# Keeping four weight blocks on chip in place of four row buffers: a 12-place gather ring for a 16-place one

## The chip, the cores and the metric

One Trainium2 chip, of which the kernel uses one core. The core has a matmul engine (TensorE, PE in the profile), a vector engine (VectorE, DVE), a scalar engine (ScalarE, ACT), GpSimd (POOL) and SyncE (SP), and 16 DMA engines that move data between HBM and the on-chip memory. The metric is the device time in microseconds of one execution, lower is better. The time of a kernel is the median of its runs.

## The reference

512 tokens of width 1024 (and 16 meta tokens ahead of them) go through two blocks, all in float32:

```python
# first block
u = rmsnorm(h, ln_mix); z, xs, bs, cs, dt, sb, sc, sx, gates = split(u @ w_in)
y_ssd = ssd_branch(z, xs, bs, cs, dt, ...)          # chunked state-space scan, group norm, @ w_out
y_sc = (sb * causal_dwconv(sc * sx, conv_w)) @ w_out_sc
g = sigmoid(gates)
h = h + (g[..., :1024] * y_ssd + g[..., 1024:] * y_sc) @ w_o
# product-key experts: 8 heads x 16 of 16384 experts for every token
q = (xb @ w_q).reshape(T, 8, 2, 128); s = einsum('thjd,hjkd->thjk', q, sub_keys)
eidx, g = top 16 of the sums of the top 16 of either half, softmax
u = expert_u[eidx]; v = expert_v[eidx]              # (T, 8, 16, 1024) each
act = gelu(einsum('td,thkd->thk', xb, u)); h = h + einsum('thk,thkd->td', g * act, v)
# second block
q, k, v, f, u = split(rmsnorm(x) @ w_in_2)
attn = forgetting_attention(q, k, v, log_sigmoid(f)); pool = multiscale_pool(u)
x = x + concat(attn, pool) @ w_out_2
x = x + (silu(h2 @ w_gate_2) * (h2 @ w_up_2)) @ w_down_2; out = rmsnorm(x)
```

Each token needs its own 128 rows of `expert_u` and of `expert_v`, 4 KB a row. For a tile of 128 tokens these are 2 x 128 gathers of 128 rows (512 KB), so 1024 gathers for the four tiles.

## The kernel before

**Stages.** The tokens are four tiles of 128. The mixer (projections and scan) runs for tile 0 and then for tiles 1 to 3. The gated sum with `w_o` ("sum") and the query with the choice of experts ("choose") run for tile 0, for tile 1, and for tiles 2 and 3 together. The second block attends tiles 0 and 1, then 2, runs the feed-forward of tiles 0 to 2, and then attends and feeds tile 3.

**One list.** `make_plan` writes one list of units (`pl.units`) by costs and due times. Each engine's program walks this list in order and issues what is its own, so the order on each engine is fixed, and only semaphore waits move it in time.

**Weights.** `Plan.load` gives each weight load a slot: `ring` (four slots, `wr0` to `wr3`, taken in turn), `early` (three slots in the first part of the buffer `rows`, for the first query), and `last` (four slots in `rows`, free after the tile-3 gathers, for attending and feeding tile 3). SP issues the loads (L1144) strictly in list order; before each it waits until the slot's last user on PE is through (PE's product named `emptied` in the plan). So a load whose slot is still in use holds all loads behind it. The gate products of a sum ask for eight blocks `wgate` (1 MB each) in each of the three sums; those with index 0 and 1 are loaded three times. The attention's products ask for six blocks `wqku` (1 MB each), in each of the three attends.

**Rows.** The gathered rows land in `ring`, a view of places of 512 KB. POOL issues the 1024 gathers (L1172) in the order of their use: `dot` (VectorE multiplies a row of `expert_u` with the token and sums, L2745), `vrow` (VectorE adds a weighted row of `expert_v`, L2769; tiles 0 and 3), and `rows` (TensorE does the same for tiles 1 and 2 with 32-wide matmuls, L1200, one unit for four gathers). A gather waits until the earlier user of its place is done. The list `slots` sets which place comes next: at first 11 places in turn (7 to 10, 5, 6, 0 to 4), and from job `narrow` on, which is reached when the experts of tile 1 are chosen, all 16. A place therefore holds the data of a gather from its issue to its use, and POOL can be at most 11, later 16 gathers ahead of the engine that uses them.

In the profile L1172 is POOL's gather, L1144 SP's weight load, L1200 most matmuls, L2745 the dots and L2769 the weighted sums. `in_pu` and `in_pv` are the expert tables, `eidxT` marks the gathers for TensorE's sums, `in_wq` the query weights, `in_wso` the output weights of the two mixer branches.

Of the kernel before, what the change touches and what calls it, by code (L numbers as in the profile page):

```python
# [15 lines left out]
NT = 4  # L16
# [3 lines left out]
NEG = -3.0e38  # L20
NW = 4
NR = 16

VEC = {}
_o = 0
# [19 lines left out]
NR0 = 11  # L45
# [9 lines left out]
PIECES = (2, 4, 1)  # L55
# [57 lines left out]
class Plan:  # L113
# [2 lines left out]

    def __init__(self):
        self.units, self.bank, self.slot, self.loads = [], {}, {}, []
        self.held = {"ring": [], "early": [], "last": []}
        self.turns = ("ring",)  # L120
        self.rings = {"lo": (0, 1, 2, 3), "hi": (4, 5, 6, 7), "two": (2,), "five": (5,)}
        self.turn = {k: 0 for k in self.rings}
        self.use = [None] * 8
        self.p = self.v = 0.0
        self.stage = None
# [12 lines left out]
    def hold(self, key, i, emptied):  # L138
        self.bank[key] = (i, self.use[i])
        self.use[i] = emptied  # L140

    def load(self, key, src, n, emptied, place=None):

        if place is None:
            place = self.turns[len(self.loads) % len(self.turns)]
        held = self.held[place]
        k = len(held)
        first, n_ = {"ring": (0, NW), "early": (NW, 3), "last": (NW + 3, 4)}[place]
        old = held[k - n_] if k >= n_ else ("dve", "h2e", NT - 1) if place == "last" else None
        held.append(emptied)  # L150
        self.slot[key] = (first + k % n_, 16 * (k // n_ + 1))
        self.loads.append((key, src, n))
        self.add("load", len(self.loads) - 1, old)
# [200 lines left out]
def plan_sum(pl, A, q):  # L354
    nt, nr, off, first = columns_of(q)
# [2 lines left out]
        pl.add("ynorm", q, 1, v=nt * vc(256))  # L358

    def gate_products(j):  # L360
        pl.load(("wgate", q, j), A["wgate"][j], 2048, ("pe", "oprod", q, j, 1))
        pl.take(("oprod", q, j, 0), "hi", ("act", "gates", q, j))
        for k in range(2):
            pl.add("oprod", q, j, k, p=mmc(nr))
            if k == 0:
                yield True
        pl.add("gates", q, j)
        yield True
# [125 lines left out]
def plan_attend(pl, A, t0, t1):  # L494
# [12 lines left out]
        yield True  # L507

    def product(s3, s_):
        if s_ == 0:  # L510
            pl.load(("wqku", t0, s3), A["wqku"][s3], 2048, ("pe", "qku", t0, s3, 1))
        pl.take(("qku", t0, s3, s_), *(("lo", ("dve" if plain else "act", "qk", t0, s3, s_)) if s3 < 4 else
                                       ("hi", ("dve", "up", t0, 2 * (s3 % 2) + s_))))
        pl.add("qku", t0, s3, s_, p=mmc(nr))
        if s3 < 4 and not (plain and s3 == 0):
            pl.add("qk", t0, s3, s_)
# [50 lines left out]
    early = t1 == NT and nt == 1  # L567
# [277 lines left out]
def build(nc, A, out):  # L845
    with ExitStack() as ctx:
        sem = lambda n: ctx.enter_context(nc.semaphore(n))
# [1 line left out]
        sb = lambda n, s, d=F32: sbx(ctx, n, s, d)  # L849
        pe, act, dve = Count(sem("pe_done")), Count(sem("act_done")), Count(sem("dve_done"))  # L850
        counts = {"pe": pe, "act": act, "dve": dve}
        landed = [sem(f"weights_landed{i}") for i in range(NW + 7)]
        gathered = [sem(f"rows_landed{i}") for i in range(NR)]
        stored = [sem(f"stored{t}") for t in range(NT)]
        x_in = [sem(f"x_landed{t}") for t in range(NT)]
# [22 lines left out]
        rows = sb("rows", [128, NR * 1024])  # L878
# [116 lines left out]
            lay(m, arena, 0, first + small + rest + [("s_sb", [128, 16, 256]), ("oh", [128, 8, 256])])  # L995
        ob = ring[9:9 + NT]
        wr += [rows[:, WSLOT * i:WSLOT * i + WSLOT] for i in range(4)]
        with ExitStack() as pk:
            kT = st[:].rearrange("p a b -> p (a b)").rearrange("p (a b) -> p a b", a=4)
            vt = sbx(pk, "vt", [128, NT, 512])  # L1000
# [101 lines left out]
        for u in pl.units:  # L1102
            if u[0] in ("dot", "vrow"):
                jobs.append(u)
            elif u[0] == "rows":
                jobs += [("row", u[1], u[2], c) for c in range(4)]
        job_of = {u: i for i, u in enumerate(jobs)}
        consumers = ("dot", "vrow", "rows")
        narrow = NR0 + sum(4 if u[0] == "rows" else 1 for u in pl.units[:pl.units.index(("chosen", 1, 1, PIECES[1] - 1))]
                           if u[0] in consumers)  # L1110
        slots, user, slot_of, before_of, value_of = [7, 8, 9, 10, 5, 6, 0, 1, 2, 3, 4], {}, [], [], []
        for i in range(len(jobs)):
            if i == narrow:
                slots = list(range(NR0, NR)) + slots
# [1815 lines left out]
```

## Time and profile before

| quantity | value |
|---|---|
| time, median of 3 runs | 2383.35 us (2379.07 to 2385.44) |
| span of the profiled execution | 2541.9 us |
| TensorE busy | 2151.2 us, 85% of the span |
| VectorE busy | 1499.3 us, 59% |
| GpSimd busy | 1020.5 us, 40% |
| ScalarE busy | 653.7 us, 26% |
| bytes moved by DMA | 839.81 MB, mean 330 GB/s |
| of these weight loads on SP's queue | 290.72 MB |

The profiled execution is longer than the timed ones: its span of 2541.9 us stands against a median of 2383.35 us, a ratio of 0.938. Positions such as "at 1268 us" are on the clock of that profiled execution, from the start of its span. The stages lie on it roughly so: mixer of tile 0 to 420 us, mixer of tiles 1 to 3 to 835, sum and query of tile 1 to 1000, sum and query of tiles 2 and 3 to 1250 (with dots and sums of tile 1 beside them), the rest of tile 1's rows to 1417, the second block beside the dots and rows of tiles 2 and 3 to 2327, and the attention and feed-forward of tile 3 to the end.

### The profile page before, as it was taken

To read this page: it belongs to the slowest core of one execution; us is meant where nothing else is said; L and a number is where in the kernel's file an instruction comes from. 1 tells how busy PE (TensorE), PEld (TensorE's weight loads), DVE (VectorE), ACT (ScalarE), POOL (GpSimd) and SP (SyncE) were. 2 spreads that over 40 slices of the span, in tenths; PEclk is the share of its full clock that TensorE was granted. 3 is DMA by queue.
4 is the path that set the end of the run, shared out by engine and by line. 5 is a ranking of instruction groups with operands and counts; after the bars stand their busy time and mean duration, and the time that the engine had idled before them with its cause. 6 is when DMAs were issued, how large, how long until landed. Compare 5 with 4: busy or idle time off the path is not lost.

```text
span 2541.9 us, 29123 instructions
## 1 busy us (share of the span) xinstructions
PE 2151.2 (85%) x10694; PEld 1516.7 (60%) x10694; DVE 1499.3 (59%) x3505; ACT 653.7 (26%) x1838; POOL 1020.5 (40%) x1028
## 2 busy tenths in 40 slices
PE   8999998999999986996675366276879799999998
PEld 7999785666666975874431254221366555545695
DVE  3441179999999368647454677710067665886321
ACT  6772235566555121001010101110122000001220
POOL 0000014555665113435566554566544544772000
PEclk8999999999998997998886567578887899999999
DMA  6767568999999978999999888999978998998485
GB/s 237 245 231 240 215 254 298 404 397 393 390 377 337 378 274 320 398 356 380 363 394 361 308 335 320 366 343 364 409 307 323 411 348 313 412 412 355 157 316 173
DMA packets 196750, 839.81 MB, mean 330 GB/s; under 512 B 22000, under 2 KB 22384, under 8 KB 164864
## 3 DMA queue, kind: packets, MB, share of 16 engines
q0 software_dynamic: 147456, 536.94, 54.8%
q1 hardware_dynamic: 43808, 290.72, 30.6%
q10 hardware_dynamic: 5344, 10.29, 1.3%
q8 instruction: 85, 1.39, 0.2%
q14 instruction: 57, 0.47, 0.0%
HBM read 835.70 MB, written 2.16 MB: 330 GB/s over the span
## 4 chain that ended last, share of the span: by engine, by line
PE 60%; DVE 15%; issue 10%; ACT 6%; POOL 5%; another core or an unknown queue 3%; DMA 2%; ACTq 0%; DVEq 0%; SPq 0%
PE ps L1200 59%; DVE rows L2745 7%; POOL rows L1172 5%; DVE ps L2769 1%; DMA rows<-in_pv,eidxT 1%; DVE h L2769 1%; DVE arena L2297 1%; DMA wr<-in_wso 1%; ACT arena L1734 1%; ACT L1871 1%; ACT arena L1865 0%; DMA wr<-in_wgate 0%; ACT L1801 0%; DVE arena L2359 0%
## 5 line engine op out<-in xcount | busy, mean ns | idle before, releaser
L1172 POOL DMA_INDIRECT rows<-in_pu,eidx x512 | 485.3, 948 | 936.6 <-DVE dots L2745 368.7
L1200 PE MATMUL ps<-arena,wr 128*128 128x128 f32 (+4 forms) x3968 | 771.9, 354 | 26.0 <-DMA wr<-in_wso 9.2
L1200 PEld LDWEIGHTS ps<-arena,wr 128*128 128x128 f32 x3968 | 606.9, 195 | 168.6 <-issue 27.3
L2745 DVE CUSTOM_DVE_ANT_0 rows<-rows,ps 128x1024 f32<-128x1024 f32 x512 | 594.0, 1217 | 11.3 <-DMA rows<-in_pu,eidx 5.5
L1200 PE MATMUL ps<-hT,wr 128*128 128x128 f32 (+2 forms) x1600 | 369.7, 390 | 44.6 <-issue 41.3
L1172 POOL DMA_INDIRECT rows<-in_pv,eidx x256 | 289.2, 1130 | 207.0 <-DVE h L2769 101.4
L1200 PEld LDWEIGHTS ps<-hT,wr 128*128 128x128 f32 x1600 | 262.5, 199 | 148.7 <-issue 57.6
L1172 POOL DMA_INDIRECT rows<-in_pv,eidxT x256 | 245.7, 960 | 142.9 <-issue 68.6
L1200 PE MATMUL ps<-rows,wz 128*32 128x512 f32 x1024 | 180.7, 778 | 78.5 <-DMA rows<-in_pv,eidxT 57.1
L1200 PE MATMUL ps<-wr,arena 128*128 128x256 f32 (+2 forms) x704 | 180.7, 412 | 2.1 <-ACT arena L1943 2.1
L2769 DVE SCALAR_TENSOR_TENSOR h<-rows,wgt,h 128x1024 f32<-128x1024 f32 x132 | 169.0, 1280 | 5.7 <-DMA rows<-in_pv,eidx 4.8
L2769 DVE SCALAR_TENSOR_TENSOR ps<-rows,wgt,ps 128x1024 f32<-128x1024 f32 x122 | 156.6, 1284 | 8.1 <-DMA rows<-in_pv,eidx 8.1
L1200 PEld LDWEIGHTS ps<-wr,arena 128*128 128x128 f32 x704 | 129.5, 192 | 49.1 <-issue 33.7
L1200 PEld LDWEIGHTS ps<-rows,wz 128*32 128x32 f32 x1024 | 39.9, 129 | 198.1 <-issue 194.2
L1200 PE MATMUL ps<-wr,fT 128*128 128x512 f32 x304 | 135.2, 602 | 5.5 <-issue 5.5
L1200 PEld LDWEIGHTS ps<-wr,fT 128*128 128x128 f32 x304 | 58.5, 193 | 80.2 <-issue 80.2
L2297 DVE SCALAR_TENSOR_TENSOR arena<-arena,vec 128x144 f32<-128x144 f32 (+2 forms) x160 | 74.8, 468 | 51.9 <-ACT arena L1794 44.7
L2401 DVE TENSOR_TENSOR arena<-arena,ps 128x256 f32<-128x256 f32 (+1 forms) x24 | 12.3, 511 | 151.2 <-PE ps L1200 146.9
L2044 ACT ACTIVATE fT<-ps 128x384 f32<-128x384 f32 (+1 forms) x44 | 16.9, 385 | 276.9 <-PE ps L1200 145.5
L2681 DVE TENSOR_TENSOR fT<-fT,ps 128x384 f32<-128x384 f32 (+1 forms) x44 | 18.5, 421 | 112.7 <-PE ps L1200 86.3
L1200 PE MATMUL ps<-arena 128*128 128x64 f32 (+3 forms) x352 | 64.5, 314 | 11.8 <-DVE arena L2356 6.6
L2633 DVE CUSTOM_DVE_ANT_0 lg<-ps,cb 128x128 f32<-128x128 f32 (+3 forms) x32 | 15.7, 492 | 93.9 <-PE ps L1200 52.2
(403 smaller groups left out, 2258.3 us busy)
## 6 DMA issues: line engine op xcount, KB each, us to landing
wr<-in_wg SPq DMA_DIRECT2D x48, 1024.0 KB
wr<-in_wgu SPq DMA_DIRECT2D x33, 1024.0 KB
wr<-in_wgate SPq DMA_DIRECT2D x24, 1024.0 KB
wr<-in_wso SPq DMA_DIRECT2D x24, 1024.0 KB
wr<-in_wq SPq DMA_DIRECT2D x16, 1152.0 KB
wr<-in_wsc SPq DMA_DIRECT2D x16, 1024.0 KB
wr<-in_wqku SPq DMA_DIRECT2D x15, 1024.0 KB
wr<-in_wdn SPq DMA_DIRECT2D x14, 1024.0 KB
```

Source lines behind the costliest of these rows:

```text
L1172: e.indirect_dma_start(ring[slot_of[i]], None, A[table], bass.IndirectOffsetOnAxis(ap=index[:, t, k:k + 1], axis=0)).then_inc(gathered[slo ...
L1200: return e.matmul(o, l, r, start=start, stop=stop, skip_group_check=True)
L1734: e.activation(dst[:, kk, col:col + w_], b[:, 128 * k:128 * k + w_], ACT.Copy, scale=gv[:, kk:kk + 1]).then_inc(*act.up("turn", tag, s, half))
L1871: e.activation(m[f"mt{c % 2}"].rearrange("p a b -> p (a b)"), fall.rearrange("p a b -> p (a b)"), ACT.Exp, scale=-1.0).then_inc(*act.up("s ...
L2044: e.activation(FD[t0]["fT"][:, j, :], b[:, 0:nr], ACT.Silu).then_inc(*act.up("silu", t0, j))
L2297: e.scalar_tensor_tensor(out=tx[:, c1:n] if k < 3 else xg[:, s_, c1:n], in0=x[:, k + c1:k + n], scalar=W["convw"][:, q4 + k:q4 + k + 1], i ...
L2401: e.tensor_tensor(flat, flat, b[:, 0:2 * nr], MUL).then_inc(*dve.up("mg", q, j))
L2633: e.tensor_tensor_reduce(m[f"lg{p}"][:, 0:kn], b[:, 0:kn], cb[:, h, 0:kn], 1.0, NEG, ADD, ALU.max, mxx[:, p:p + 1]).then_inc(*dve.up("fron ...
L2681: e.tensor_tensor(fT[:, j, :], fT[:, j, :], b[:, 0:nr], MUL).then_inc(*dve.up("fT", t0, j))
L2745: e.tensor_tensor_reduce(row, row, wide[:], 1.0, 0.0, MUL, ADD, dots[:, k:k + 1]).then_inc(*dve.up(*u))
L2769: e.scalar_tensor_tensor(out=sum_, in0=row, scalar=wgt[:, k:k + 1], in1=sum_, op0=MUL, op1=ADD).then_inc(*dve.up(*u))
```

## The change

Two new slots (`kept`) are laid over places 7 to 10 of the row ring (`rows[:, 7168:11264]`). In them lie `wgate` 0 and 1, loaded once for all three sums, and, when the last sum has used them, `wqku` 0 and 1, loaded once for all three attends. The weight loads fall from 294 to 286; eight loads of 1024 KB are gone. For this the row ring gives up the four places: it runs over 7 places before `narrow` and over 12 after it. The index of the job `narrow` is 294 for 298. The fourth `last` slot lies over the first kept one, so its first load waits for the last product with `wqku` 0 and no longer for the norm ahead of tile 3.

```diff
+KEPT = 2
@@ class Plan
+    def keep(self, key, src, n, last):
+        first = (key[0], 0) + key[2:]
+        if first in self.slot:
+            self.slot[key] = self.slot[first]
+        else:
+            self.load(key, src, n, last, "kept")
@@ Plan.load
-        first, n_ = {"ring": (0, NW), "early": (NW, 3), "last": (NW + 3, 4)}[place]
-        old = held[k - n_] if k >= n_ else ("dve", "h2e", NT - 1) if place == "last" else None
+        first, n_ = {"ring": (0, NW), "early": (NW, 3), "last": (NW + 3, 4), "kept": (NW + 7, KEPT)}[place]
+        old = held[k - n_] if k >= n_ else None
+        if place == "last" and k < n_:
+            old = ("pe", "qku", NT - 1, 0, 1) if k == 3 else ("dve", "h2e", NT - 1)
@@ gate_products
-        pl.load(("wgate", q, j), A["wgate"][j], 2048, ("pe", "oprod", q, j, 1))
+        if j < KEPT:
+            pl.keep(("wgate", q, j), A["wgate"][j], 2048, ("pe", "oprod", 2, j, 1))
+        else:
+            pl.load(("wgate", q, j), A["wgate"][j], 2048, ("pe", "oprod", q, j, 1))
@@ product (attention)
-        if s_ == 0:
+        if s_ == 0 and s3 < KEPT:
+            pl.keep(("wqku", t0, s3), A["wqku"][s3], 2048, ("pe", "qku", NT - 1, s3, 1))
+        elif s_ == 0:
             pl.load(("wqku", t0, s3), A["wqku"][s3], 2048, ("pe", "qku", t0, s3, 1))
@@ the weight slots
         wr += [rows[:, WSLOT * i:WSLOT * i + WSLOT] for i in range(4)]
+        wr += [rows[:, 7168 + 2048 * i:7168 + 2048 * i + 2048] for i in range(KEPT)]
@@ the row ring
-        narrow = NR0 + sum(...)
+        narrow = NR0 - 2 * KEPT + sum(...)
-        slots, user, slot_of, before_of, value_of = [7, 8, 9, 10, 5, 6, 0, 1, 2, 3, 4], {}, [], [], []
+        slots, user, slot_of, before_of, value_of = [5, 6, 0, 1, 2, 3, 4], {}, [], [], []
```

The order of the computing instructions is the same on TensorE, VectorE and ScalarE, and so is the order of the 1024 gathers on POOL; the places of the gathers, and with them the waits, differ. What moves is SP's row of weight loads. On SP, in front of the query of tile 1 and the sum of tiles 2 and 3, before:

```order
L1144 DMA wr0<-in_wq 128x2304
L1144 DMA wr1<-in_wq 128x2304
L1144 DMA wr2<-in_wgate 128x2048
L1144 DMA wr3<-in_wq 128x2304
L1144 DMA wr0<-in_wq 128x2304
L1144 DMA wr1<-in_wq 128x2304
L1144 DMA wr2<-in_wq 128x2304
L1144 DMA wr3<-in_wgate 128x2048
L1144 DMA wr0<-in_wq 128x2304
L1144 DMA wr1<-in_wq 128x2304
L1144 DMA wr2<-in_wso 128x2048
L1144 DMA wr3<-in_wso 128x1024
```

and after:

```order
L1161 DMA wr0<-in_wq 128x2304
L1161 DMA wr1<-in_wq 128x2304
L1161 DMA wr2<-in_wq 128x2304
L1161 DMA wr3<-in_wq 128x2304
L1161 DMA wr0<-in_wq 128x2304
L1161 DMA wr1<-in_wq 128x2304
L1161 DMA wr2<-in_wq 128x2304
L1161 DMA wr3<-in_wq 128x2304
L1161 DMA wr0<-in_wso 128x2048
L1161 DMA wr1<-in_wso 128x1024
```

The two gate blocks of the coming sum no longer stand between the query's loads, and each query load takes a slot that comes free earlier. On SP, at the end of the query of tiles 2 and 3, before:

```order
L1144 DMA wr2<-in_wq 128x2304
L1144 DMA wr3<-in_wq 128x2304
L1144 DMA wr0<-in_wqku 128x2048
L1144 DMA wr1<-in_wqku 128x2048
L1144 DMA wr2<-in_wqku 128x2048
L1144 DMA wr3<-in_wqku 128x2048
L1144 DMA wr0<-in_wqku 128x2048
L1144 DMA wr1<-in_wqku 128x2048
```

and after:

```order
L1161 DMA wr0<-in_wq 128x2304
L1161 DMA wr1<-in_wq 128x2304
L1161 DMA rows<-in_wqku 128x2048 x2
L1161 DMA wr2<-in_wqku 128x2048
L1161 DMA wr3<-in_wqku 128x2048
L1161 DMA wr0<-in_wqku 128x2048
L1161 DMA wr1<-in_wqku 128x2048
```

The first two attention blocks go to the kept slots, which wait for nothing that is still to come, so six blocks are issued where four were before the ring was full.

## Rows read from the trace of the kernel before

**Rows 1.** Busy time by stretch: us, each engine (instructions), granted clock, DMA share, GB/s

```profile
420.00:840.00 420.00, 401.87 (x1685) 281.94 (x1683) 392.50 (x624) 240.85 (x694) 241.13 (x228) 0.97 0.99 384
938.00:1008.00 70.00, 40.68 (x244) 36.82 (x242) 57.59 (x210) 10.93 (x24) 32.36 (x34) 0.80 0.84 322
1310.00:1417.00 107.00, 61.92 (x312) 13.73 (x305) 61.06 (x293) 2.63 (x7) 74.97 (x75) 0.71 0.97 368
1640.00:1800.00 160.00, 107.31 (x531) 35.78 (x531) 22.79 (x67) 15.86 (x44) 102.03 (x109) 0.78 0.96 358
2160.00:2300.00 140.00, 139.24 (x377) 69.91 (x376) 120.25 (x104) 3.95 (x7) 104.14 (x91) 1.00 1.02 412
```

**Rows 2.** The page: the chain that ended last, shares of the span by engine

```profile
PE 60%; DVE 15%; issue 10%; ACT 6%; POOL 5%; another core or an unknown queue 3%; DMA 2%; ACTq 0%; DVEq 0%; SPq 0%
```

**Rows 3.** Gathers in 420 to 800 us: POOL's idle time before them, by releaser

```profile
  DVE dots L2745: 60.0, 54
  DVE h L2769: 45.9, 19
```

**Rows 4.** Order of time, VectorE, 424 to 440 us: start, duration, instruction

```profile
423.97 1.22 DVE L2745 CUSTOM_DVE_ANT_0 rows<-rows,ps 128x1024 f32<-128x1024 f32 x1
...
431.94 1.22 DVE L2745 CUSTOM_DVE_ANT_0 rows<-rows,ps 128x1024 f32<-128x1024 f32 x1
...
436.51 1.22 DVE L2745 CUSTOM_DVE_ANT_0 rows<-rows,ps 128x1024 f32<-128x1024 f32 x1
```

**Rows 5.** Order of time, POOL, from 1352.9 us: the last gather of a unit

```profile
1353.42 0.94 POOL L1172 DMA_INDIRECT rows<-in_pv,eidxT  x1 [0.30 <-issue]
```

**Rows 6.** Order of time, TensorE, from 1352.9 us: the unit that used it

```profile
1359.78 2.79 PE L1200 MATMUL ps<-rows,wz 128*32 128x512 f32 x12 [5.32 <-DMA rows<-in_pv,eidxT]
```

**Rows 7.** Order of time, TensorE, 938 to 1012 us, in tile 1's query

```profile
979.37 5.88 PE L1200 MATMUL ps<-rows,wr 128*128 128x128 f32 x32 [4.62 <-DMA wr<-in_wq]
...
996.69 3.72 PE L1200 MATMUL ps<-arena,wr 128*128 128x256 f32 x16 [1.07 <-DMA wr<-in_wso]
...
1008.00 4.32 PE L1200 MATMUL ps<-arena,wr 128*128 128x256 f32 x12 [6.70 <-DMA wr<-in_wso]
```

**Rows 8.** Order of time, TensorE, 834 to 850 us, at tile 1's sum

```profile
840.11 5.62 PE L1200 MATMUL ps<-arena,wr 128*128 128x128 f32 x48 [1.46 <-DMA wr<-in_wso]
846.43 3.84 PE L1200 MATMUL ps<-arena,wr 128*128 128x128 f32 x32 [0.69 <-DMA wr<-in_wgate]
```

**Rows 9.** Order of time, POOL, 1246 to 1275 us, gathers for TensorE's sums

```profile
1260.06 0.94 POOL L1172 DMA_INDIRECT rows<-in_pv,eidxT  x1 [0.53 <-remote]
...
1268.64 0.94 POOL L1172 DMA_INDIRECT rows<-in_pv,eidxT  x1 [3.90 <-PE ps L1200]
```

**Rows 10.** Order of time, TensorE, 1246 to 1275 us, tile 1's weighted sums (x16 is a unit)

```profile
1272.42 1.92 PE L1200 MATMUL ps<-rows,wz 128*32 128x512 f32 x16
```

**Rows 11.** Order of time, 1308 to 1322 us, both engines

```profile
1308.97 0.95 POOL L1172 DMA_INDIRECT rows<-in_pv,eidxT  x1 [7.40 <-PE ps L1200]
...
1314.56 3.48 PE L1200 MATMUL ps<-rows,wz 128*32 128x512 f32 x16 [2.47 <-issue]
```

**Rows 12.** Gathers in 1310 to 1410 us: who waited for them (us, times)

```profile
  PE ps L1200: 42.2, 15
```

**Rows 13.** SP's queue in order of time, 1236 to 1330 and 1500 to 1520 us

```profile
1238.79 12.23 SPq L1144 DMA_DIRECT2D wr<-in_wq  x2
...
1503.31 7.24 SPq L1144 DMA_DIRECT2D wr<-in_wqku  x2
```

**Rows 14.** Order of time, POOL, 1652 to 1680 us, tile 2's gathers

```profile
1664.65 0.94 POOL L1172 DMA_INDIRECT rows<-in_pv,eidxT  x1 [4.99 <-PE ps L1200]
...
1670.09 0.94 POOL L1172 DMA_INDIRECT rows<-in_pv,eidxT  x1 [0.77 <-PE ps L1200]
```

**Rows 15.** Order of time, TensorE, 1652 to 1680 us, tile 2's weighted sums

```profile
1675.52 1.92 PE L1200 MATMUL ps<-rows,wz 128*32 128x512 f32 x16
```

**Rows 16.** Weighted sums of tile 3, 2160 to 2330 us: VectorE's idle time before them

```profile
  DMA rows<-in_pv,eidx: 12.9, 11
```

More of the change, by code:

```diff
@@ L118, in __init__ @@
         self.units, self.bank, self.slot, self.loads = [], {}, {}, []
-        self.held = {"ring": [], "early": [], "last": []}
+        self.held = {"ring": [], "early": [], "last": [], "kept": []}
         self.turns = ("ring",)
@@ L851, in build @@
         counts = {"pe": pe, "act": act, "dve": dve}
-        landed = [sem(f"weights_landed{i}") for i in range(NW + 7)]
+        landed = [sem(f"weights_landed{i}") for i in range(NW + 7 + KEPT)]
         gathered = [sem(f"rows_landed{i}") for i in range(NR)]
@@ L1108, in build @@
         consumers = ("dot", "vrow", "rows")
-        narrow = NR0 + sum(4 if u[0] == "rows" else 1 for u in pl.units[:pl.units.index(("chosen", 1, 1, PIECES[1] - 1))]
+        narrow = NR0 - 2 * KEPT + sum(4 if u[0] == "rows" else 1 for u in pl.units[:pl.units.index(("chosen", 1, 1, PIECES[1] - 1))]
                            if u[0] in consumers)
-        slots, user, slot_of, before_of, value_of = [7, 8, 9, 10, 5, 6, 0, 1, 2, 3, 4], {}, [], [], []
+        slots, user, slot_of, before_of, value_of = [5, 6, 0, 1, 2, 3, 4], {}, [], [], []
         for i in range(len(jobs)):
```

## The prediction, made before the changed kernel was run

> **What bounds the kernel now.** I read the table of stretches first, to see which engine is full where. Between 420 and 840 us three things are full at once: TensorE 402 of 420 us, VectorE 393, and the DMA engines 99% busy at 384 GB/s. In tile 1's query (938 to 1008 us) TensorE is at 41 of 70 us. In the two stretches of weighted sums on TensorE (1310 to 1417, 1640 to 1800) it is at 58% and 67% while the DMA engines are at 0.97 and 0.96; from 2160 to 2300 us it is full again, 139 of 140, with VectorE at 120 [rows 1]. The chain that ended last agrees: PE has 60% of it, VectorE 15%, DMA as such only 2% [rows 2]. So the kernel is bound by TensorE where it is fed, and by the stream of gathered rows where TensorE sums them. Bytes count only where something waits for them, and so does the row ring's depth.
>
> Next come the waits at the ring. In 420 to 800 us POOL waited for a dot 54 times and for a weighted sum 19 times [rows 3]: the ring was full, and POOL as far ahead as it may be. That is what the change takes from.
>
> All terms below are in time of the profiled execution. Its span is 2541.9 us against a median of 2383.35, so a sum in the span is multiplied by 0.938.
>
> **How far ahead the ring must be.** A gather costs POOL 0.94 us and 0.30 us between two, 1.25 us in a row. The last of a unit's four was issued from 1353.42 to 1354.36 [rows 5], and the TensorE unit that waited for it started at 1359.78 [rows 6]: 5.4 us from the end of the issue to use. A place is thus out of use for at least 0.30 + 0.94 + 5.4 = 6.6 us. At the mean pace of the mixer stretch, 228 gathers in 420 us [rows 1] or 1.8 us a row, seven places are 12.5 us, and enough. In bursts they aren't quite.
>
> **The mixer, ring of 7 for 11.** The change takes four places for the kept gates from the start. At 424 us VectorE does eleven dots within 13.7 us: the first at 423.97, the seventh at 431.94, the last from 436.51 to 437.7 [rows 4]. With 11 places all eleven rows can lie ready. With 7, the eighth dot (433.1 us) needs the place of the first, free at 425.2: 425.2 + 6.6 = 431.8, which is in time by 1.3 us. The ninth to eleventh follow at POOL's 1.25 us, against 1.14 from dot to dot. The 5.4 us were measured in a stretch where few weights load. If landing takes 2 to 3 us more in the mixer, with DMA at 0.99, each burst stalls VectorE by 1 to 2 us, and VectorE idles only 27 of 420 us there [rows 1], so that a part of it reaches TensorE. The 228 rows of the stretch are some 20 such bursts; at a third of a us each that is 7 us. Low end 0 (all hidden), high end 20 (a full us each). I take +7, nearer to the low end, since the one burst that I can work out is covered.
>
> **The sum of tile 1: the kept gates.** TensorE waited 1.46 us for `wso` and 0.69 us for `wgate` there [rows 8]. With two of eight gate blocks already on chip SP's row is two loads shorter and both waits can go: −2 (−3 to 0).
>
> **The query of tile 1.** Two gate loads stand between the query loads, and four waits in turn hold them. TensorE waited 4.62 us for `wq`, 1.07 and 6.70 us for `wso` [rows 7]. Without the gates each query load takes a slot that is free one product earlier, so the first two waits should go. The last is a load that waits for a slot of a late query product, in the new order too; it stays. −5.7, and a little behind it: −6. High gain −12 (6.70 goes too), low 0 (a ScalarE result is what comes next).
>
> **Tile 1's weighted sums, ring of 12 for 16.** One unit uses four gathers, so POOL may be three units ahead for four. At 1260.06 POOL starts the four gathers of a unit, and at 1268.64, after a wait of 3.90 us for PE, those of the next [rows 9]. The wait at 1268.64 is for the fourth unit back. In the new ring the unit issued at 1260.06 waits for that same one, so it starts at 1268.64: its last gather is issued by 1268.64 + 3 x 1.25 + 0.94 = 1273.3 and is there at 1278.7. TensorE ran this unit at 1272.42 [rows 10]. +6.3. The same happens at 1308.97, where POOL had waited 7.40 us: the unit that TensorE starts at 1314.56 [rows 11] would be issued only from there, its last gather by 1313.7, there at 1319.1: +4.5. Behind it TensorE is already waiting for rows, 42.2 us in 15 waits [rows 12], and POOL issues without a pause; there the depth of the ring changes nothing more. A stream that goes from ahead to behind loses the four places once, 4 x 1.25 = 5.0 us, which is the size of both. Sum +10.8 (5 to 13).
>
> **Two more weight loads in the way.** The first two `wqku` blocks are issued right behind the query's last loads, which end at 1251.0 us; before, the last two of the six came at 1503 [rows 13], and now all six fall ahead of that. 2.1 MB at 368 GB/s [rows 1] are 5.7 us of the DMA engines just ahead of the stretch in which TensorE waits for rows. Taken at half, since gathers of POOL don't fill the engines by themselves: +3 (0 to 5.7).
>
> **Tile 2's dots and sums, and tile 3's.** Dots of tile 2: VectorE has slack; +2 (0 to 4). Sums of tile 2: at 1664.65 and 1670.09 POOL waits for PE [rows 14]. One unit's shift puts the unit used at 1675.52 [rows 15] behind the release at 1670.09: last issue by 1674.8, there at 1680.2, +4.7 (2 to 8). Tile 3's sums on VectorE already waited 12.9 us for rows in 11 waits [rows 16]; four places less cost it up to 5.0 us once, of which TensorE, 139 of 140 us busy [rows 1], sees what its next product that needs VectorE can't wait out: +4 (0 to 7).
>
> **The rest.** The four `wqku` blocks saved in the second and third attends were never waited for. The new wait of the fourth `last` slot holds only SP, with loads for tile 3's attention queued behind it, 10 us or more ahead of use: 0.
>
> Sum: 7 − 2 − 6 + 6.3 + 4.5 + 3 + 2 + 4.7 + 4 = **+23.5 us** of 2541.9, times 0.938 = +22.0: **2405 us**.
>
> **A page against a row.** The landing of 5.4 us decides five of the terms. The Trainium skill, "DMA: Bandwidth & Descriptors", section "Anatomy of one DMA — SWDGE (gpsimd) path", fits a transfer from GpSimd as 2.0 us plus bytes over 436,000 bytes per us; for 524,288 bytes that is an estimate of 3.2 us, and the rows show 5.4. By the page the ring of 7 would be ample. I stay with the row, which has this kernel's traffic in it. The rival "light rows" below is what a landing of about the page's size would do.
>
> **The rivals.**
> *Fewer bytes win (faster).* The DMA engines are at 0.96 to 1.02 in every stretch but the query [rows 1]; if transfers as such set the pace, 8 blocks of 1.05 MB, 8.4 MB at 384 GB/s, are 21.8 us less, half of it where rows are waited for. With the −8 of sum and query and no loss at the ring: −19, times 0.938: 2366 us. It decides if landing times shrink with the traffic so that 12 places carry what 16 did. Against it: four of the blocks go from stretches where no one waits for weights, the DMA engines moved 412 GB/s from 2160 to 2300 and 384 in the mixer, so that 384 is no ceiling, and the work at 1268.64 and 1308.97 waits by the order of units, not by traffic. Beside this, the same page, in "Where 436 GB/s comes from", puts the limit of HBM reads at about 358 GB/s a core; the 412 contradicts it as a ceiling here, and with it that every byte counts. Chance 0.10.
> *Even.* Landing is short in the mixer, VectorE's stalls stay on VectorE, and one of the two stalls in tile 1's sums is filled by other units: losses of 8 against gains of 8: 2383 us. Chance 0.15.
> *Light rows.* A row's landing is shorter where the stream isn't behind: midway between the 1.3 us that 0.52 MB take at 412 GB/s and 5.4, so 3.3 us. Then tile 1's stalls are 4.2 and 2.4, tile 2's 2.6, tile 3's 2, the mixer's and the dots' 0, the early blocks 3: −8 + 14.2 = +6.2, times 0.938: 2389 us. Only the one row of 5.4 speaks against it. Chance 0.07.
> *The mixer stalls in earnest.* Landing there takes 8 us or more; the pace of seven places is then (8 + 1.2 + 1.2) / 7 = 1.5 us a row, each burst loses over 1 us, and TensorE follows: +20 for +7, the other terms at their upper ends (13, 5.7, 4, 8, 7) less 8: +50, 2430 us. Chance 0.16.
> *The forecast*, 2393 to 2420 us: chance 0.52.
>
> **How the numbers follow.** About 0.3% is what a measurement of this kernel can tell from no change: 2376 to 2390. Faster by more is the first rival, with the lower edge of the even case: 0.11. Within it: the even case, light rows and no more, less that edge: 0.20. Slower: forecast and stalling mixer, 0.69. For 8 in 10 the range runs from 2379, just under the even case, to 2432, just over the stalling mixer; what is left out is the fast rival below and the worst tenth above.
>
> **What would show it.** In the new profile: POOL's waits for PE around 1250 to 1310 grow from four short ones to one a unit, and TensorE waits for `rows<-in_pv,eidxT` there two times, some 5 us each (right), or its busy share in the stretch stays (wrong). VectorE gets waits for `rows<-in_pu` in 420 to 840, about 10 us in all; none at all means the mixer term is 0. The waits of 4.62 and 1.07 us for weights in tile 1's query vanish and that of 6.70 stays. The prediction is wrong in sign if the stretches of weighted sums take no longer while the query loses its waits, and wrong in size mainly through the landing time in the mixer.

## The result

The changed kernel takes 2435.72 us (median of 4 runs, 2426.5 to 2439.56) against 2383.76 us before: a ratio of 1.021, 95% interval 1.0184 to 1.0237, so 52 us slower. The forecast was 2405 us with a range up to 2432. The sign was right; the size was less than half of what was measured, and the time lies outside the range. One of the four runs of the kernel with only the early ring cut, told of below, took 2827.79 us at a granted clock of 0.726 and is left out of every number here.

### A second profile of before

The execution profiled for [rows 1] to [rows 16] was 158 us longer than its timed runs. A second profile of the same program has a span of 2378.2 us, and its timed runs agree (2383.64 us, ratio 1.0013, 0.9992 to 1.0034). It is the one to lay beside the changed kernel. The page of the second profile of before: the span, the busy time by engine, and the chain that ended last.

```profile
span 2378.2 us, 29123 instructions
...
PE 2077.9 (87%) x10694; PEld 1480.3 (62%) x10694; DVE 1501.1 (63%) x3505; ACT 652.3 (27%) x1838; POOL 1016.5 (43%) x1028
...
PE 54%; DVE 20%; DMA 9%; issue 6%; POOL 6%; ACT 6%; ACTq 0%; DVEq 0%
```

The page of the changed kernel, the same lines:

```profile
span 2437.7 us, 29111 instructions
...
PE 2101.6 (86%) x10694; PEld 1491.3 (61%) x10694; DVE 1507.9 (62%) x3505; ACT 651.4 (27%) x1838; POOL 1013.1 (42%) x1028
...
PE 46%; DVE 23%; DMA 14%; POOL 6%; ACT 6%; issue 5%; ACTq 0%; DVEq 0%
```

Busy time hardly moved; waiting did. The chain has 14% of its length in DMA for 9%, and 23% in VectorE for 20%. The first profile showed only 2% for DMA [rows 2]. Two things differ there. TensorE was slower (busy 2151 us for 2078), and its idle time before the units that sum rows was shorter. And that trace holds no landing time for any of the 1024 gathers, so a part of the waits for rows stands under other names: its chain has 10% "issue" and 3% "another core or an unknown queue", where the second profile has 6% and none. The groups of these units in the first and in the second profile (busy, mean ns | idle before):

```profile
L1200 PE MATMUL ps<-rows,wz 128*32 128x512 f32 x1024 | 180.7, 778 | 78.5 <-DMA rows<-in_pv,eidxT 57.1
L1200 PE MATMUL ps<-rows,wz 128*32 128x512 f32 x1024 | 157.7, 745 | 98.5 <-DMA rows<-in_pv,eidxT 97.3
```

The idle time itself is 78.5 us for 98.5; only 57.1 of the 78.5 was put down to rows. The waits of the second profile of before, over the whole span (engine, what it waited for: us, times, longest):

```profile
PE ps L1200 <- DMA rows<-in_pv,eidxT: 97.3, 43, 8.1
POOL rows L1172 <- PE ps L1200: 44.2, 23, 6.1
DVE rows L2745 <- DMA rows<-in_pu,eidx: 35.5, 29, 3.4
```

and of the changed kernel:

```profile
PE ps L1217 <- DMA rows<-in_pv,eidxT: 105.8, 44, 8.1
POOL rows L1189 <- PE ps L1217: 64.8, 31, 6.2
DVE rows L2762 <- DMA rows<-in_pu,eidx: 49.2, 38, 3.4
```

So VectorE and TensorE waited for rows before the change too, in more places than the first profile let see, and a shorter ring makes POOL wait more (44.2 to 64.8 us behind TensorE) and the users of the rows too.

### Where the time went

VectorE has the same 3505 instructions in the same order in all kernels here, so the start of one and the same instruction can be compared between traces. The growth of each stretch over the second profile of before, in us (the third column is the ring of the changed kernel with the loads of before, the next two cut one ring only; they are told of below):

| stretch (us in the second profile of before) | changed | ring 7, 12 | early 7 | late 12 | forecast |
|---|---|---|---|---|---|
| mixer, tiles 1 to 3 (414 to 807) | +17.0 | +15.9 | +16.9 | 0.0 | +7 |
| sum and query of tile 1 (807 to 1017) | −2.4 | −1.3 | −1.7 | −3.8 | −8 |
| tile 1's dots beside the next sum (1017 to 1144) | +8.1 | +10.5 | +9.6 | +3.4 | none |
| tile 1's sums on TensorE (1144 to 1376) | +10.4 | +5.1 | −3.5 | +3.6 | +10.8, +3 |
| tile 2's dots (1376 to 1563) | −1.2 | +8.1 | +0.2 | +8.5 | +2 |
| tile 2's sums (1563 to 1774) | +6.5 | +6.5 | +0.2 | +6.4 | +4.7 |
| 1774 to 1998 | +16.1 | +7.0 | +9.3 | +14.3 | none |
| tile 3's sums on VectorE (1998 to 2192) | +7.4 | +9.3 | +0.4 | +8.4 | +4 |

The rest lies within 2.4 us at the start and 0.0 at the end. In the mixer these profiles agree well: all kernels with 7 places and full loads have +15.9 to +17.1, all with 11 have 0.3 us or less. The stretch from 1774 us on needs a word: +16.0 of its +16.1 come between 1799 and 1851 us, where TensorE's granted clock dips. The kernel with only the early ring cut has a like dip and +9.3 us there, though its ring is the full one by then, so 9.3 of the 16.1 are taken to be the clock. Its trace by tens of us (each engine's busy time, granted clock, DMA share, GB/s), in that place:

```profile
1822.00:1832.00 10.00, 10.00 (x31) 6.71 (x30) 5.26 (x15) 3.25 (x9) 2.67 (x4) 0.50 0.99 394
1832.00:1842.00 10.00, 9.13 (x41) 8.54 (x41) 6.58 (x15) 2.18 (x6) 3.13 (x4) 0.50 0.64 199
```

and the second profile of before:

```profile
1810.00:1820.00 10.00, 9.12 (x28) 4.47 (x28) 9.74 (x20) 2.08 (x3) 6.73 (x8) 1.00 1.02 406
1820.00:1830.00 10.00, 10.00 (x35) 6.37 (x34) 8.60 (x16) 1.15 (x2) 6.57 (x7) 1.00 1.02 417
```

The granted clock is 0.50 there, the lower level of 1.2 GHz, for 24 us, against 1.00. Beside the first profile there are thirteen: nine have the dip for 24 to 27 us, two for 7 us (one of them is the kernel of the third column), two not at all. The first profile of before has it for 27 us and the second, of the same program, has none, so it is not fixed by the program; what sets it off is open. The timed runs of the kernel before scatter by 20 us with a granted clock from 0.924 to 0.938. Less 9.3 us the changed kernel's profile is 50 us longer, near the 52 of the timed runs.

### The profile page after: what moved, and what is told of

The parts are those of the page before. It is cut to its first block, busy times and chain, and to the rows that moved or that the text cites. A ratio compares the mean times of both kernels' runs of the same rounds, so it can differ in the third digit from the quotient of the medians.

```text
span 2437.7 us, 29111 instructions
## 1 busy us (share of the span) xinstructions
PE 2101.6 (86%) x10694; PEld 1491.3 (61%) x10694; DVE 1507.9 (62%) x3505; ACT 651.4 (27%) x1838; POOL 1013.1 (42%) x1028
## 4 chain that ended last, share of the span: by engine, by line
PE 46%; DVE 23%; DMA 14%; POOL 6%; ACT 6%; issue 5%; ACTq 0%; DVEq 0%
PE ps L1217 45%; DVE rows L2762 12%; POOL rows L1189 6%; DMA rows<-in_pu,eidx 5%; DMA rows<-in_pv,eidxT 4%; DMA rows<-in_pv,eidx 4%; DVE h L2786 1%; DVE arena L2314 1%; DVE ps L2786 1%; DMA wr<-in_wgate 1%; ACT arena L1751 1%; DVE rows L2226 1%; ACT L1888 0%; ACT arena L1882 0%; DVE rows L2224 0%
## 5 line engine op out<-in xcount | busy, mean ns | idle before, releaser
L1217 PE MATMUL ps<-arena,wr 128*128 128x128 f32 (+4 forms) x3776 | 740.5, 356 | 17.5 <-DMA wr<-in_wso 10.1
L1217 PEld LDWEIGHTS ps<-arena,wr 128*128 128x128 f32 x3776 | 577.3, 194 | 158.6 <-issue 17.9
L2762 DVE CUSTOM_DVE_ANT_0 rows<-rows,ps 128x1024 f32<-128x1024 f32 x512 | 601.8, 1217 | 53.2 <-DMA rows<-in_pu,eidx 49.2
L1217 PE MATMUL ps<-hT,wr 128*128 128x384 f32 (+2 forms) x1440 | 323.1, 385 | 5.7 <-DVE fT L2698 4.2
L1217 PEld LDWEIGHTS ps<-hT,wr 128*128 128x128 f32 x1440 | 228.2, 192 | 97.4 <-DVE fT L2698 4.8
L1217 PE MATMUL ps<-rows,wz 128*32 128x512 f32 x1024 | 163.9, 770 | 107.1 <-DMA rows<-in_pv,eidxT 105.8
L2786 DVE SCALAR_TENSOR_TENSOR ps<-rows,wgt,ps 128x1024 f32<-128x1024 f32 x122 | 156.7, 1284 | 13.7 <-DMA rows<-in_pv,eidx 13.6
L1217 PE MATMUL ps<-hT,rows 128*128 128x128 f32 (+1 forms) x608 | 84.8, 301 | 21.1 <-DVE xx L2612 20.4
L1217 PEld LDWEIGHTS ps<-hT,rows 128*128 128x128 f32 x608 | 79.8, 203 | 24.5 <-issue 18.6
L2061 ACT ACTIVATE fT<-ps 128x384 f32<-128x384 f32 (+1 forms) x44 | 16.9, 384 | 261.9 <-PE ps L1217 201.2
```

Source lines behind the costliest of these rows:

```text
L1217: return e.matmul(o, l, r, start=start, stop=stop, skip_group_check=True)
L2061: e.activation(FD[t0]["fT"][:, j, :], b[:, 0:nr], ACT.Silu).then_inc(*act.up("silu", t0, j))
L2762: e.tensor_tensor_reduce(row, row, wide[:], 1.0, 0.0, MUL, ADD, dots[:, k:k + 1]).then_inc(*dve.up(*u))
L2786: e.scalar_tensor_tensor(out=sum_, in0=row, scalar=wgt[:, k:k + 1], in1=sum_, op0=MUL, op1=ADD).then_inc(*dve.up(*u))
```

## The experiments

### Which ring, and what the kept blocks give

The ring of the changed kernel, with the old loads, leaves places 7 to 10 unused:

```diff
-        narrow = NR0 + sum(...)
-        slots, ... = [7, 8, 9, 10, 5, 6, 0, 1, 2, 3, 4], ...
+        narrow = NR0 - 4 + sum(...)
+        slots, ... = [5, 6, 0, 1, 2, 3, 4], ...
```

> The row ring of the changed kernel (7 places, then 12) with the weight loads of the kernel before; the four places lie unused. Theory A (the lost places cost more than I had them, the kept blocks give back about 8 us): slower than the changed kernel, 2440 to 2450 us, +57 to +65 over before. Theory B (the ring costs the 22 to 30 us that I had, and the loss beyond it comes from the kept blocks: early attention blocks in the way of the rows, or the order of the loads): 2405 to 2415 us, well under the changed kernel's 2436.

Measured: 2447.11 us, ratio 1.0281 (1.0258 to 1.0305), +64. Theory A, near its upper end.

Cutting the early ring alone adds places 7 to 10 back at `narrow` (`slots = list(range(NR0 - 4, NR)) + slots`):

> Only the early ring is cut, 7 places for 11; the late one has all 16, the loads are those of before. By my sum the mixer's term alone: +7 us of span, 2390 us. Theory A with the mixer mis-sized: +15 to +20 us, 2400 us. If the early ring is long enough (its places wait less than the dots need): 2384 us.

Measured: 2409.5 us (three runs), ratio 1.0112 (1.0081 to 1.0144), +26. More than either number that I had.

Cutting the late ring alone takes them out there (`+ [s for s in slots if s not in (7, 8, 9, 10)]`):

> Only the late ring is cut, 12 places for 16; the early one has its 11, the loads are those of before. By my sum 6.3 + 4.5 + 2 + 4.7 + 4 = 21.5 us of span, about 2404 us. Theory A with the late terms mis-sized: +35 to +45 us, 2420 to 2430 us. If only one of the two cuts matters, this and the run with the early ring cut tell which; if their losses add up to that of both cuts, the stages don't share it.

Measured: 2421.22 us, ratio 1.0171 (1.0148 to 1.0195), +38. The losses add up: 26 + 38 = 64 for 64. The kept blocks give back 2447.1 − 2435.7 = 11 us beside the short rings. The second profile of before, for the record of the expectation:

> The kernel before once more, for a second profile of it. The first profiled execution was 158 us longer than its timed ones; this one should show where. Every theory expects a ratio of 1.000 within 0.2%. If the profiled span is near 2382 us, it is the one to lay beside the changed kernel's 2437.7.

It came out at 2378.2 us of span, as told above.

### What the kept blocks give by themselves

The kernel before with its full rings, and no transfer for the eight repeated loads; their products read a constant tile instead, so its output is of other numbers:

```diff
+        if j < 2 and q > 0:
+            pl.slot["wgate", q, j] = (NW + 7, 0)
+        else:
             pl.load(("wgate", q, j), A["wgate"][j], 2048, ("pe", "oprod", q, j, 1))
...
+        if s_ == 0 and s3 < 2 and t0 > 0:
+            pl.slot["wqku", t0, s3] = (NW + 7, 0)
+        elif s_ == 0:
             pl.load(("wqku", t0, s3), ...)
...
+        wr.append(Same(con))
```

> The gain side by itself. The kernel before with its full rings (11, then 16 places), in which the eight repeated loads are simply left out: the products of gate blocks 0 and 1 in the second and third sums, and of attention blocks 0 and 1 in the second and third attends, take their weights from a constant tile instead (so those products are of other numbers; nothing else differs). Theory A (a saved transfer is worth only what someone waited for): the query's waits of 4.4 and 1.2 us and part of the sum's 3.3, 2378 to 2381 us, -4 to -7. Theory B (bytes count, since the DMA engines are full): 8.4 MB at 400 GB/s are 21 us, half or more of which shows, 2363 to 2373 us. If the waits only move to the next load: 2384 us.

Measured: 2379.35 us, ratio 0.9986 (0.9968 to 1.0005): −3 us, no change that can be told. Theory A fits, and so does "the waits only move"; the interval, +1 to −8 us, leaves both. Theory B (−11 us or more), and with it my rival "fewer bytes win", falls. So on the full rings, with memory that costs nothing, the kept blocks could bring 8 us at the very most. The waits of TensorE for weights in tile 1's query say why. In the second profile of before:

```profile
959.15 5.46 PE L1200 MATMUL ps<-rows,wr 128*128 128x128 f32 x32 [4.38 <-DMA wr<-in_wq]
...
976.22 3.72 PE L1200 MATMUL ps<-arena,wr 128*128 128x256 f32 x16 [1.24 <-DMA wr<-in_wso]
...
988.45 23.82 PE L1200 MATMUL ps<-arena,wr 128*128 128x256 f32 x97 [7.62 <-DMA wr<-in_wso]
```

and in the changed kernel:

```profile
994.62 5.70 PE L1217 MATMUL ps<-arena,wr 128*128 128x256 f32 x17 [8.97 <-DMA wr<-in_wso]
```

The first two waits are gone, as forecast from [rows 7], and the third stayed and took up 1.3 us more. 13.2 us of waiting became 9.0. At tile 1's sum nothing was won: three waits of 3.3 us together in the second profile of before, three of 2.5 in the changed kernel and of 2.4 with the same ring and the old loads.

Keeping the gates only, and giving their places back to the ring once the last sum has used them (7, then 11, then 16 places):

```diff
+        mid = NR0 - 2 * KEPT + sum(... units before ("oprod", 2, 1, 1) ...)
...
+            if i == mid:
+                slots = [7, 8, 9, 10] + slots
```

> Half of the change: the two gate blocks are kept, the attention blocks are loaded as before, and the four places go back to the row ring as soon as the last sum has used the gates (7 places, then 11, then 16). By the parts so far: +27 of the early ring less what the kept gates give, which the profiles put at 3 to 4 us in tile 1's query (waits of 4.4, 1.2 and 7.6 us for weights become one of 9.0): 2405 to 2409 us. If the gates' 4 MB less traffic counts by itself in the mixer and the sums, 2395 us or less. If returning the places earlier than the choice of tile 1's experts matters, 2400.

Measured: 2403.31 us, ratio 1.008 (1.0054 to 1.0106). That is 6 us better than the early ring cut alone, though the intervals overlap, so the stretches must tell; its mixer is +17.1 like the others', and the dots from 1017 to 1144 us are at −0.1 where all the others with 7 places have +6.5 to +10.5. So that second loss, which my sum did not have, is the short ring too. It is an after-effect. The wider ring begins with the job `narrow`, whose gather is issued at 1022.9 us in the second profile of before and within 2 us of that point of VectorE's work in the others, while the loss comes from 1037 to 1090 us. But the early ring sets how far ahead POOL is when the long run of gathers begins. Job 288 is issued at 999.0 us with 11 places, at 1009.3 on the same clock with 7, and at 999.7 with the places handed back. Behind `narrow` POOL issues a gather every 1.25 us almost without a pause, and until it is ahead again VectorE waits. Its idle time before these dots (us, times), in the second profile of before, with 7 early places, and with the places handed back:

```profile
  DMA rows<-in_pu,eidx: 5.4, 5
  DMA rows<-in_pu,eidx: 13.0, 9
  DMA rows<-in_pu,eidx: 1.9, 2
```

### Why seven places are too few

Two places more:

> An early ring of 9 places (between the 7 that cost 27 us and the 11 of before), 16 later, loads as before. If the loss is proportional to the places: half, 2397 us. If 11 is well over what is needed and 7 just under it (bursts of dots longer than the ring), most is won back by two places: 2385 to 2390 us. If the ring is still too short at 11, the loss is nearly linear or more, 2395 to 2400.

Measured: 2392.39 us, ratio 1.0032 (1.0008 to 1.0056), +8 of the 26. By this interval (+2 to +13 us) alone half the loss could not be told from a quarter. The stretches can tell: in the mixer it is +1.3 us for +16.9, and from 1017 to 1144 us +1.2 for +9.6. In these two stretches the loss is not proportional to the places; there is a knee between 7 and 9. The chain of the changed kernel, followed back through its mixer, starts with these pieces (start, us, what):

```profile
413.10 9.72 DMA rows<-in_pu,eidx
422.85 1.22 DVE rows L2762
424.35 9.87 DMA rows<-in_pu,eidx
434.25 1.22 DVE rows L2762
```

A row takes 9.7 and 9.9 us there from the start of its gather; from the end of the gather, as I had measured 5.4 [rows 5, 6], that is 8.8 and 8.9. Nine places' worth of dots at 1.14 us are 10.3 us, about what such a row needs; seven, 8.0 us, are not. To see whether the weights' traffic makes the rows late, the mixer's weight loads for tiles 1 to 3 were halved, in the kernel before and in the one with 7 early places (the other half of each block is left out, so the products read there what the slot held before):

```diff
+                    if key[0] in ("wg", "wsc") and key[1] == 1:
+                        n //= 2
+                        src = src[:, 0:n]
                     e.dma_start(wr[slot][:, 0:n], src).then_inc(landed[slot], 16)
```

> The pair for the next run: the kernel before, but the mixer's weight loads for tiles 1 to 3 bring only the first half of their columns (the products read what was there before in the other half, so the numbers differ; instructions and waits are the same). Stage from the first dots in the mixer to its end (393.0 us in the second profile of before): all theories expect 390 to 393 us, since nothing waited for these loads.

> The kernel with an early ring of 7 places, with the same halved weight loads. The stage was 17 us longer than before with full loads. Theory L (7 places are too few because a row lands late, behind the weights' traffic; a place's round is landing plus 2.4 us, and 7 rounds of 10 to 12 us are at or over the 1.8 us a row that the stage takes): with half the weights the rows land earlier and the growth over the pair falls to 0 to 6 us. Theory P (POOL's pace of one gather in 1.25 us after each burst limits, whatever the landing): the growth stays at 13 to 17 us.

Measured, one execution of each, in the stretch from the mixer's first dots to its end: 392.8 us with 11 places and 398.8 with 7, a growth of 6.0 us where full loads gave 16.9. Two thirds of the loss went with half of the weights: theory L, at the top of its bounds. Whether the 6 us left are the other half of the weights or something else is not shown. The gathers of the dots in the first 190 us of that stretch (count, median us from the start of the gather to landing; the traces hold the landing of about half of them or more) say the same. Before, second profile:

```profile
rows<-in_pu,eidx POOLq DMA_INDIRECT x106, 10.2
```

seven early places with full loads, and then with half loads:

```profile
rows<-in_pu,eidx POOLq DMA_INDIRECT x110, 9.0
```

```profile
rows<-in_pu,eidx POOLq DMA_INDIRECT x108, 6.7
```

VectorE's idle time before the dots there (us, times), with full loads and with half:

```profile
  DMA rows<-in_pu,eidx: 8.0, 10
```

```profile
  DMA rows<-in_pu,eidx: 0.5, 1
```

With 11 places a landing of 10.2 us is longer than with 7, and does no harm: VectorE has no wait for rows there. With 7 places it falls to 9.0, and still VectorE waits. Over the whole mixer the changed kernel's VectorE waits 8.7 us for rows before dots and 3.9 before weighted sums, both from nothing.

### The late ring, and the two loads ahead of tile 1's rows

> A late ring of 14 places between the 12 that cost 38 us and the 16 of before. Proportional: 2402 us. The sums on TensorE use four places a unit, so 14 places let POOL be three units ahead and half of a fourth. If whole units decide, 14 is little better than 12 for tiles 1 and 2: 2410 us; if rows decide, 2395 to 2402.

Measured: 2394.17 us, ratio 1.0036 (1.0018 to 1.0055), +9 of the 38. Half the places cost a quarter of the loss (the interval is +4 to +13 us); it bends as well, less sharply. That is the reading "rows decide", just under its 2395; whole units do not.

In the changed kernel TensorE waits for the first rows of this stretch right behind the new `wqku` loads (order of time, TensorE's sums in the changed kernel):

```profile
1253.06 3.64 PE L1217 MATMUL ps<-rows,wz 128*32 128x512 f32 x16 [4.93 <-DMA rows<-in_pv,eidxT]
1258.18 3.32 PE L1217 MATMUL ps<-rows,wz 128*32 128x512 f32 x16 [1.48 <-DMA rows<-in_pv,eidxT]
1263.30 1.92 PE L1217 MATMUL ps<-rows,wz 128*32 128x512 f32 x16 [1.80 <-DMA rows<-in_pv,eidxT]
1268.42 1.92 PE L1217 MATMUL ps<-rows,wz 128*32 128x512 f32 x16 [2.11 <-DMA rows<-in_pv,eidxT]
```

With only the late ring cut, and the old loads, the same units:

```profile
1229.64 3.08 PE L1200 MATMUL ps<-rows,wz 128*32 128x512 f32 x16 [3.20 <-DMA rows<-in_pv,eidxT]
1234.76 3.64 PE L1200 MATMUL ps<-rows,wz 128*32 128x512 f32 x16 [2.04 <-DMA rows<-in_pv,eidxT]
```

10.3 us of waits for 5.2. To test it, the kept blocks became the last two of the six, loaded when tile 1's sums are over:

```diff
-        if s_ == 0 and s3 < KEPT:
-            pl.keep(("wqku", t0, s3), A["wqku"][s3], 2048, ("pe", "qku", NT - 1, s3, 1))
+        if s_ == 0 and s3 >= 4:
+            pl.keep(("wqku", t0, s3), A["wqku"][s3], 2048, ("pe", "qku", NT - 1, s3, 1), ("pe", "rows", 1, 31))
```

> The changed kernel, but the two attention blocks that are kept are the last of the six (4 and 5) instead of the first, and they are loaded only when TensorE has done tile 1's last sum, not right behind the query's loads. If the two extra megabytes in front of tile 1's row stream cost what the profiles say (8.0 us of growth from 1220 to 1266 us against 3.2 with the old loads), this is 4 to 5 us faster than the changed kernel: 2430 to 2432 us. If the growth there has another cause: 2436 us. If the later load is missed at the start of the attention, slower.

Measured: 2444.21 us, ratio 1.0264 (1.0237 to 1.0292): 8 us slower than the changed kernel by the medians, with intervals that just touch, and in no case faster. The local part held: from 1144 to 1376 us the growth is 4.5 us for the changed kernel's 10.4, near the 5.1 of the short rings with the old loads. But tile 2's dots, which cost the changed kernel nothing, now cost 7.9 us, as in the two kernels with a short late ring and the old loads (8.1 and 8.5). What was won in one place was given back in the next. In the kernel with only the late ring cut VectorE waits for the dots' rows there, and SP brings four blocks within some 40 us (SP's queue, order of time; the second `wqku` at 1442.57, the second `wv` at 1456.4):

```profile
1415.49 27.41 SPq L1144 DMA_DIRECT2D wr<-in_wqku  x2
1449.48 7.23 SPq L1144 DMA_DIRECT2D wr<-in_wv  x2
```

and the idle time before the dots from 1440 to 1473 us:

```profile
  DMA rows<-in_pu,eidx: 5.9, 4
```

The changed kernel has its six attention blocks by then, and only the two `wv` loads fall there:

```profile
1478.04 7.24 SPq L1161 DMA_DIRECT2D wr<-in_wv  x2
```

The kernel just told of has four blocks again. Its attention blocks come early, but the rest of SP's queue moves up behind them: one `wv` at 1438.92 us, then, within 14 us, the other (1463.0) and two `wout`:

```profile
1438.92 24.43 SPq L1163 DMA_DIRECT2D wr<-in_wv  x2
1469.92 7.24 SPq L1163 DMA_DIRECT2D wr<-in_wout  x2
```

The kernel below that keeps one block has three, the `wqku` ahead of the wait being gone:

```profile
1445.62 0.33 SPq L1161 DMA_DIRECT2D wr<-in_wqku  x1
1452.53 7.24 SPq L1161 DMA_DIRECT2D wr<-in_wv  x2
```

It has −0.6 us in those dots, where the same 14 places with the old loads, and four blocks, have +2.7. So in all six kernels with a short late ring the loss goes with the number of blocks in these 40 us: four in the four that lose, three and two in the two that don't. With all 16 places four blocks do no harm. No run changed this number alone, so it fits and is not shown.

### Half the change

> The change at half its size: one block kept (gate 0, then attention 0), rings of 9 and then 14 places. If the parts add up, +7.6 for the early ring of 9 and +9.4 for the late one of 14, less half of the 11 us that the kept blocks gave beside the short rings: 2394 to 2398 us. If a kept block gives its gain mostly with the first of the two: 2388 to 2392. Faster than before only if the rings' losses are not additive.

Measured: 2401.13 us, ratio 1.0074 (1.0045 to 1.0102), +17: above both ranges expected, though the interval (+11 to +24 us) reaches into the first. The two losses add up (8 + 9), and the one kept block gives nothing that shows. From 1017 to 1144 us this kernel has +4.6, where 9 early places by themselves have +1.2; that is left open. No kernel that takes places from the rings beats the one before, and none of this kind is to be expected to: 3 us (8 by the end of the interval) is what there was to win with two blocks, and two places of either ring cost as much.

## Why the prediction was wrong, step by step

The mechanism was right in kind: a shorter ring makes POOL issue late, and the users of the rows wait. What failed is the size of the mixer's term and two stretches left out of the sum. The sum was +23.5 us of the span and the profiles have +50 without the dip: the mixer is 10.0 of the difference, tile 1's dots 8.1, the stretch from 1774 us 6.8, the gain of sum and query 5.6; the other terms together take off 4.

- **What bounds the kernel.** Right in kind, wrong in degree. The row stream was taken as a bound only in the two stretches of sums on TensorE. The profile that I read had TensorE at a lower clock (0.65 from 1417 to 1640 us; the second profile has 0.74 for the like stretch), shorter waits for rows (idle time of 78.5 us for 98.5 before TensorE's sums, of 11.3 for 38.3 before the dots), and no landing times, so that only 57 and 5.5 us of these showed as waits for rows. The 2% of DMA in the chain was read as it stood, with 10% "issue" and 3% unknown beside it. Multiplying by 0.938 at the end took off another 1.5 us.
- **The mixer, +7.** This is the step that failed most: +17.0. It took the landing of one row in a stretch with few weights, 5.4 us from the end of the gather [rows 5, 6], and the lower third of its own bounds, 0 to 20. The two rows of the chain have 8.8 and 8.9 us on the same measure. The mechanism was right: bursts of dots, and landing behind weights, borne out by the pair with half loads; and VectorE's waits for rows before dots, foretold as about 10 us, are 8.7. The rival "the mixer stalls in earnest" (landing of 8 us or more, +20, 2430 us) had this term nearly right. It came closest as a whole too, but in part by luck: it took the other losses at their upper ends and had nothing for the two stretches left out.
- **Tile 1's dots.** Left out of the sum. The early ring was priced in the mixer only, but it also sets how far ahead POOL is when the run of gathers behind `narrow` begins, and the dots there cost +8.1 with it and −0.1 with the places handed back.
- **The sum and query of tile 1, −8.** −2.4 measured, and some of that is scatter (the kernel with the late ring cut has −3.8 and the old loads). The first two waits went and the last stayed, as foretold, but it took back 1.3 us, and the sum won nothing. The free blocks on full rings show −3 us for the whole kernel.
- **Tile 1's sums, +6.3 and +4.5.** The ring alone costs 3.6 to 5.1 us there. With only the late ring cut, the first unit of these sums starts 2.8 us ahead of the second profile of before (1189.6 for 1192.4), the unit of the forecast's first stall 0.2 us ahead (1240.34 for 1240.54), and that of its second stall 0.2 too (1281.9 for 1282.1): a first loss of 2.6 us, and none at the second. That this stretch, +13.8 forecast with the next term, came to +10.4 is in part luck: the ring was taken too dear and the loads too cheap.
- **Two more loads in the way, +3.** About +5 (10.4 for 5.1). Right in kind, and inside its bounds of 0 to 5.7; moving them away gave 5.9 us back there. The halving had no ground: from 1310 to 1417 us of the first profile POOL's gathers alone took 94.2% of the 16 DMA engines.
- **Tile 2's dots, +2.** −1.2 in the changed kernel; but +8 with the short late ring and the old loads. Here the kept blocks earned most of what they did, 9 us. I had given them 0 outside of tile 1's sum and query.
- **Tile 2's sums, +4.7, and tile 3's, +4.** +6.5 and +7.4. Right in kind, both low; in the kernel with the full late ring they are +0.2 and +0.4. At tile 3's weighted sums VectorE's waits for rows grew from 12.5 to 15.8 us, so they show less than half of the 7.4.
- **Between, 1774 to 1998.** Nothing forecast; +6.8 once the dip of the clock is taken off, and +7.0 with the short rings and the old loads, of which a dip of 7 us may be a part. Tile 3's dots run there from the ring of 12.
- **The rest.** The new wait of the fourth `last` slot cost nothing: from 2192 us on the growth is 0.0.

The Trainium skill, "DMA: Bandwidth & Descriptors", section "Anatomy of one DMA — SWDGE (gpsimd) path", gave an estimate of 3.2 us for a landing. That was farther off than the one row of 5.4, in the same direction: from the start of the gather, so with its 0.94 us, the medians were 9.0 and 10.2 us in the mixer, and 6.7 even with half of the weights away.

## What to carry to other kernels

A ring of landing buffers can have a knee. In the mixer here it held as long as its places, at the pace of a burst (9 x 1.14 = 10.3 us), covered the time that a row takes there (about 10 us), and cost 17 us when they did not (8.0 us). Take the landing from the stretch in question, under its traffic, and price the ring also in the stretch behind the one where it is short: the lead that it leaves is the next stretch's start. Bytes that nobody waits for were worth little, even where the DMA engines show 99%: the saved eight megabytes were 3 us, 8 by the end of the interval. And look first whether the profiled execution is like the timed ones, and whether it has the landing times of its transfers; one that ran at a lower clock and had none hid the very waits that the change lengthens.

## What the runs showed that I had not expected

- Dropping 8.4 MB of 840 with nothing else touched changed the time by 3 us (0.9986, 0.9968 to 1.0005), with the DMA engines at a share of 1.02 from 1017 to 2108 us of the second profile.
- Nine places are nearly as good as eleven in the mixer (+1.3 us), seven are not (+16.9).
- With fewer places rows land sooner: over the same stretch a median of 10.2 us with 11 places, 9.6 with 9 and 9.0 with 7; over the whole kernel 13.6 us for the dots' rows before and 9.6 in the changed kernel. That this pays a part of a shorter ring's cost is likely and was not tested.
- A dip of the granted clock to 0.50 for 24 us in full work goes with 9.3 to 9.4 us in the six profiles with at least 14 late places and a dip of that length, and two of thirteen profiles do not have it at all.
- The share of a wait that a profile names can be a matter of its records: with no landing times, 57 of 78.5 us of idle time were put down to rows, with them 97.3 of 98.5.
